# Stick-breaking attention on one core: scores as two products per key block instead of three, and later-key sums taken from softplus tiles that VectorE adds first

## The reference, cut to what matters

```python
def stick_breaking_attention(q, k, v):
    for i in range(S // Q_BLOCK):            # 4 blocks of 128 queries
        L = (i + 1) * Q_BLOCK
        z = jnp.einsum('bhqd,bhkd->bhqk', qb, kb) * inv_sqrt
        mask = s_idx < t_idx
        log1m = jnp.where(mask, -jax.nn.softplus(z), 0.0)
        after = lax.cumsum(log1m, axis=3, reverse=True) - log1m   # sum over the later keys
        logw = jax.nn.log_sigmoid(z) + after
        w = jnp.where(mask, jnp.exp(jnp.where(mask, logw, 0.0)), 0.0)
        outs.append(jnp.einsum('bhqk,bhkd->bhqd', w, vb))
```

## Time and profile before

| | us |
|---|---|
| median of 3 runs | 1657.78 (1657.31 to 1659.21) |
| the profiled execution, its own time | 1656.84 |
| its span, from the first to the last instruction | 1655.0 |
| PE busy (matmul) | 1628.8, 98% of the span |
| DVE busy | 1050.5 |
| ACT busy | 766.2 |
| POOL busy | 732.0 |

### The profile page before, as it was taken

The page is one execution under the profiler, slowest core; times in us unless marked ns, Lnnn a source line. Parts: engine busy times, 40 slices in busy tenths (PEclk is TensorE's granted clock), DMA queues, the critical chain, the costliest instruction groups (busy, mean ns, idle before and its releaser), DMA issues.

```text
span 1655.0 us, 24390 instructions
## 1 busy us (share of the span) xinstructions
PE 1628.8 (98%) x9460; PEld 1399.6 (85%) x9460; DVE 1050.5 (63%) x1396; ACT 766.2 (46%) x1029; POOL 732.0 (44%) x540
## 2 busy tenths in 40 slices
PE   7999999999999999999999999999999999999997
PEld 4787899999988898888888887887888789999887
DVE  6777758999920065578778788775113699996102
ACT  4756455455543355334444546544223445544322
POOL 3342343333376635443543434445444443335663
PEclk9999999999999999999999999999999999999999
DMA  8565223333243333233332323223233323332432
GB/s 290 208 225 179 91 89 115 115 105 115 86 150 105 108 115 121 98 102 102 102 105 87 119 85 115 90 90 97 95 112 119 126 83 117 112 111 82 150 97 68
DMA packets 65127, 193.49 MB, mean 117 GB/s; under 512 B 5984, under 2 KB 8288, under 8 KB 64000
## 3 DMA queue, kind: packets, MB, share of 16 engines
q1 hardware_dynamic: 65024, 192.06, 35.3%
HBM read 183.59 MB, written 8.45 MB: 116 GB/s over the span
## 4 chain that ended last, share of the span: by engine, by line
PE 90%; DVE 7%; ACT 1%; issue 1%; DMA 1%; SPq 0%; DVEq 0%
PE PR L778 18%; PE PR L779 18%; PE PR L784 18%; PE PR L1182 4%; PE PR L1189 4%; PE PR L1184 4%; PE AX L1182 3%; PE AX L1189 3%; PE AX L1184 3%; PE PR L795 1%; PE PR L796 1%; PE PR L794 1%; PE AX L1003 1%; PE AX L1330 1%; PE AX L1334 1%
## 5 line engine op out<-in xcount | busy, mean ns | idle before, releaser
L703 POOL TENSOR_TENSOR wlo<-raw,whi 128x512 fp32r<-128x512 f32 (+1 forms) x456 | 605.8, 1354 | 631.3 <-ACT whi L1461 631.3
L1461 ACT ACTIVATE whi<-raw 128x1024 fp32r<-128x1024 f32 x216 | 225.9, 1052 | 150.0 <-PE PR L784 127.2
L778 PE MATMUL PR<-h3h,whi 128*128 128x512 f32 x608 | 245.5, 404 | 0.0
L779 PE MATMUL PR<-h3l,whi 128*128 128x512 f32 x608 | 240.4, 395 | 0.0
L722 POOL TENSOR_TENSOR wlo<-raw,whi 128x512 fp32r<-128x512 f32 x72 | 119.1, 1675 | 239.8 <-ACT whi L1719 239.8
L784 PE MATMUL PR<-h3h,wlo 128*128 128x512 f32 x608 | 154.2, 395 | 0.0
L1182 PE MATMUL PR<-ch,whi 128*128 128x256 f32 x560 | 136.0, 282 | 2.0 <-DVE gate L2509 1.2
L784 PEld LDWEIGHTS PR<-h3h,wlo 128*128 128x128 f32 x608 | 114.2, 188 | 27.6
L778 PEld LDWEIGHTS PR<-h3h,whi 128*128 128x128 f32 x608 | 114.3, 188 | 26.6 <-issue 1.2
L779 PEld LDWEIGHTS PR<-h3l,whi 128*128 128x128 f32 x608 | 114.4, 188 | 26.4 <-issue 1.0
L1184 PE MATMUL PR<-cl,whi 128*128 128x256 f32 x560 | 135.7, 281 | 0.0
(11 more groups left out here) (480 smaller groups left out, 3619.2 us busy)
## 6 DMA issues: line engine op xcount, KB each, us to landing
raw<-w SPq DMA_DIRECT2D x224, 512.0 KB, 3.4
cond<-wcond SPq DMA_DIRECT2D x48, 512.0 KB, 4.2
raw<-w SPq DMA_DIRECT2D x32, 384.0 KB, 3.2
raw<-w SPq DMA_DIRECT2D x32, 320.0 KB, 2.9
x_keep<-x SPq DMA_DIRECT2D x3, 2048.0 KB, 7.3
x<-x_keep SPq DMA_DIRECT2D x2, 2048.0 KB, 8.4
abc_a<-acum_rows SPq DMA_DIRECT2D x8, 512.0 KB, 3.9
abc_b<-acum_rows SPq DMA_DIRECT2D x8, 512.0 KB, 4.5
```

The lines of the kernel that those rows point to most:

```text
L703: ins = pool.tensor_tensor(wlo[:, j, a:a + n], raw[:, j, a:a + n], whi[:, j, a:a + n], ALU.subtract)
L778: pe.matmul(bank, whi[:, j, w], part_of(oh, k0 + k), start=first and i == 0, stop=False)
L779: pe.matmul(bank, whi[:, j, w], part_of(ol, k0 + k), start=False, stop=False)
L1461: act.activation(whi[:, j, :], raw[:, j, :], ACT.Copy).then_inc(hi_ready, 1)
```

## The change

1. **Rounded keys twice on the partitions.** `kh` becomes `kk` (`kk_even`, `kk_odd`, one [128, 2, 512] tile for each buffer): for head e of the pair, `kk[:, e, :]` holds the rounded keys on the head's own 64 partitions and, copied, on the other 64. `qh` and `ql` become `qq`: `qq[:, e, :]` holds the rounded queries on the head's own 64 partitions and the low queries on the other 64. One matmul over 128 partitions is then high times high plus high times low. The low keys times the rounded queries stay a matmul over 64 partitions. `scores` issues all 128-partition matmuls of a part and then all 64-partition ones.
2. Each tile that was written by one instruction on 128 partitions is written by two on 64 (`in_result`, `qk_low`, `whole_q_low` and the first key and query tiles), and ACT has two more copies for each key tile, with a semaphore `kk_ready` that `scores` waits for.
3. **Later-key sums.** DVE adds softplus tiles after part 0 (`later_sums`): block 2 plus block 3 for the last 128 queries (128 columns at `SUM_1`), and then two 128-column sums with block 1 (256 columns). `az`, `sp`, `sph` and `spl` are longer by 384 columns; ACT rounds these (one more instruction per head), and DVE takes their low part (one more). `later_keys` then uses a sum where it used two or three blocks.

```diff
@@ scores
-                p, r = h // 2, slice(64 * (h % 2), 64 * (h % 2) + 64)
-                pe.wait_ge(qkl_ready, 2 if p == 0 else lows(nth("k", p)))
+                p, e = h // 2, h % 2
+                pe.wait_ge(kk_ready, p + 1)
+                pe.wait_ge(qkl_ready, 4 if p == 0 else 2 * lows(nth("k", p)))
...
                     for j, c in blocks:
-                        for i, (ks, qs) in enumerate(((kh, qh), (kh, ql), (kl, qh))):
-                            mm = pe.matmul(AXf[:, c:c + T - j * P], ks[r, p % 2, j * P:(j + 1) * P], qs[r, p % 2, j * P:T],
-                                           start=j != 3 and i == 0, stop=False, skip_group_check=True)
+                        pe.matmul(AXf[:, c:c + T - j * P], kk[p % 2][:, e, j * P:(j + 1) * P], qq[p % 2][:, e, j * P:T],
+                                  start=j != 3, stop=False, skip_group_check=True)
+                    for j, c in blocks:
+                        mm = pe.matmul(AXf[:, c:c + T - j * P], kl[rows_of(e), p % 2, j * P:(j + 1) * P],
+                                       qq[p % 2][rows_of(e), e, j * P:T], start=False, stop=False, skip_group_check=True)
                     mm.then_inc(z_done, 1)
@@ later_keys
-                for n, (_, _, blocks) in enumerate(PARTS):
-                    for part, ready in ((sph, sph_ready), (spl, spl_ready)):
-                        pe.wait_ge(ready, 2 * h + n + 1)
-                        for j, c in blocks:
-                            mm = pe.matmul(AXf[:, c:c + T - j * P], late[:, 2, :], part[:, c:c + T - j * P],
...
-                            for j2 in range(j + 1, NCH):
-                                c2, off = KCOL[j2], c + (j2 - j) * P
-                                mm = pe.matmul(AXf[:, off:off + T - j2 * P], late[:, 3, :], part[:, c2:c2 + T - j2 * P],
...
+                for part, ready in ((sph, sph_ready), (spl, spl_ready)):
+                    pe.wait_ge(ready, 2 * h + 1)
+                    for j, c in PARTS[0][2]:
+                        add(c, T - j * P, 2, part[:, c:c + T - j * P], stop=part is spl and j == NCH - 1)
+                    add(KCOL[2] + P, P, 3, part[:, KCOL[3]:KCOL[3] + P], stop=part is spl)
+                for part, ready in ((sph, sumh_ready), (spl, suml_ready)):
+                    pe.wait_ge(ready, h + 1)
+                    mm = add(KCOL[1] + P, 2 * P, 3, later_1(part), stop=part is spl)
+                mm.then_inc(cum_done, 1)
+                pe.wait_ge(sph_ready, 2 * h + 2)
+                add(0, T, 2, sph[:, 0:T])
+                add(P, P, 3, sph[:, KCOL[1]:KCOL[1] + P])
+                for part in (sph, spl):
+                    add(2 * P, 2 * P, 3, part[:, SUM_0:SUM_0 + 2 * P])
+                add(P, P, 3, spl[:, KCOL[1]:KCOL[1] + P])
+                pe.wait_ge(spl_ready, 2 * h + 2)
+                mm = add(0, T, 2, spl[:, 0:T], stop=True)
+                mm.then_inc(cum_done, 1)
@@ act, before head 0
-            act.activation(kh[:, 0, :], PR[:, 1, :], ACT.Identity, bias=bias[:, 1:2]).then_inc(qkvu_ready, 1)
+            for e in range(2):
+                ins = act.activation(k_high(0, e), PR[rows_of(e), 1, :], ACT.Identity, bias=bias[rows_of(e), 1:2])
+            ins.then_inc(qkvu_ready, 1)
             h1_high(6)
             h1_high(7)
+            act.wait_ge(qkvu_ready, 1)
+            for e in range(2):
+                ins = act.activation(k_high(0, e, other=True), k_high(0, e), ACT.Copy)
+            ins.then_inc(kk_ready, 1)
@@ act, in_result
+                if kind == 1:
+                    act.wait_ge(qkvu_ready, u + 1)
+                    for e in range(2):
+                        ins = act.activation(k_high(p, e, other=True), k_high(p, e), ACT.Copy)
+                    ins.then_inc(kk_ready, 1)
@@ act, soft
                     act.activation(sph[:, c:c + w], sp_[:, c:c + w], ACT.Copy).then_inc(sph_ready, 1)
+                    if n == 0:
+                        act.wait_ge(later_sum, 2 * h + 2)
+                        act.activation(sph[:, SUM_1:NZL], sp_[:, SUM_1:NZL], ACT.Copy).then_inc(sumh_ready, 1)
@@ dve, soft_plus
+                    if n == 0:
+                        dve.wait_ge(sumh_ready, h + 1)
+                        dve.tensor_tensor(spl[:, SUM_1:NZL], sp_[:, SUM_1:NZL], sph[:, SUM_1:NZL], ALU.subtract).then_inc(
+                            suml_ready, 1)
+            def later_sums(h):
+                dve.wait_ge(sp_ready, 2 * h + 1)
+                dve.tensor_tensor(sp_[:, SUM_1:SUM_1 + P], sp_[:, KCOL[2] + P:NZ], sp_[:, KCOL[3]:KCOL[3] + P],
+                                  ALU.add).then_inc(later_sum, 1)
+                dve.wait_ge(later_sum, 2 * h + 1)
+                dve.tensor_tensor(sp_[:, SUM_0:NZL].rearrange("p (a b) -> p a b", a=2),
+                                  sp_[:, KCOL[1] + P:KCOL[1] + 3 * P].rearrange("p (a b) -> p a b", a=2), later_1(sp_),
+                                  ALU.add).then_inc(later_sum, 1)
```

More of the change, by code:

```diff
@@ L193, in hybrid_blocks @@
             ff2 = sb("ff2", [P, 2, T], F32, over)
+        with ExitStack() as over:
+            kk_odd = sb("kk_odd", [P, 2, T], F32R, over)
         abc_a = sb("abc_a", [P, 2, T])
@@ L207, in hybrid_blocks @@
         rr = sb("rr", [P, T])
+        with ExitStack() as over:
+            pw_odd = sb("pw_odd", [P, NZ - T], F32, over)
         sq = sb("sq", [P, 2, T])
@@ L240, in phase_a @@
                      pooled=a("pooled", [P, T]), wp=a("wp", [P, 4, P]))
-            t.update(ql=a("ql", [P, 2, T], F32R), kl=a("kl", [P, 2, T], F32R),
-                     pw_odd=a("pw_odd", [P, NZ - T]), pfix=a("pfix", [P, 16]), shifts=a("shifts", [P, KT, 2], F32R), bias=a("bias", [P, 8]))
+            t.update(qq_odd=a("qq_odd", [P, 2, T], F32R), kl=a("kl", [P, 2, T], F32R),
+                     pfix=a("pfix", [P, 16]), shifts=a("shifts", [P, KT, 2], F32R), bias=a("bias", [P, 8]))
             return t.values()
-        (mix1, h1h, xn, h1l, mixh, mixl, cond, macc, att, late, az, sp_, sph, spl, qh, kh, vT, vtok, pw, padA, padB, padC, pooled, wp,
-         ql, kl, pw_odd, pfix, shifts, bias) = region(phase_a)
+        (mix1, h1h, xn, h1l, mixh, mixl, cond, macc, att, late, az, sp_, sph, spl, qq_even, kk_even, vT, vtok, pw, padA, padB, padC, pooled, wp,
+         qq_odd, kl, pfix, shifts, bias) = region(phase_a)
+        kk, qq = (kk_even, kk_odd), (qq_even, qq_odd)
         def phase_joint(a):
@@ new lines, in add @@
+                def add(to, w, weights, moving, stop=False):
+                    return pe.matmul(AXf[:, to:to + w], late[:, weights, :], moving, start=False, stop=stop, skip_group_check=True)
+                for part, ready in ((sph, sph_ready), (spl, spl_ready)):
[3 more added lines that the diff above has]
+                    add(KCOL[2] + P, P, 3, part[:, KCOL[3]:KCOL[3] + P], stop=part is spl)
```

60 lines of the change are left out of this document (42 added, 18 removed).

## The result

The changed kernel takes 1662.2 us (median of 9 runs, 1660.41 to 1662.94), the kernel before 1657.59 (9 runs, 1656.22 to 1659.27). The ratio is 1.0028, with a 95% interval of 1.0019 to 1.0036: **slower by 4.6 us**, where the prediction took 3.3 us for what a measurement tells from no change. The forecast was 1660.4, no change. The time lies in its range, but over its own bound for slower (1661.1), to which it gave 0.28, and the loss of 2.6 us was 2 us short.

The account below looks back on a forecast made before the run. The prediction took PE's own instructions to bound attention (57 to 190 us). Losses of 8.65 us less gains of 6.1 gave +2.6: 1659.4 for the profiled execution, 1660.4 for the median, range 1655.0 to 1663.8.

Parts of the forecast that it names:

- PE's gains: PE in attention: 0.57 us per head in later keys plus 1.5 over eight heads in scores, 6.1 us in all.
- changes inside a head are free: Rival: shape changes inside a head's scores cost PE nothing, 4.7 us less on PE; about 1657; chance 0.10.
- changes cost double: Rival: shape changes in scores cost double, or 128-row matmuls behind 64 read PSUM late; about 1663.5; chance 0.10.
- Half the partitions, half the price: Rival: split ACT and DVE instructions on 64 partitions cost half, so early losses shrink; about 1655.4; chance 0.10.
- First loss, before head 0: Before head 0, split tiles and key copies make the last h1l tile late; PE loses 1.8 us.
- Second loss, head 0: Head 0: PE waits 1.5 us for sph, 0.55 for spl and 0.9 for the weights at head 1's scores.
- Third loss, head 1: Head 1's later keys: DVE delivers spl late, PE loses 1.2 us, then 0.3 for weights.
- Heads 2 to 5: Slack of 2 to 3 us between low part and use, no waits; PE wins back 3.1 us.
- Pooled tiles: The last two pool_map: DVE delivers pooled tiles 2 and 3 late, PE loses 1.0 and 0.9 us.
- Weights of heads 5 and 6: Next scores after the shorter later keys of heads 5 and 6 wait for weights, 0.2 + 0.3 = 0.5 us.
- Nothing waits: Rival: copies and halves hide beside PE's units, so all 6.1 us are won; 1651.7; chance 0.08.
- DVE the bound in every head: Rival: 1.3 us more DVE work per head makes split lows late in every head; 1667; chance 0.12.

Follow-up runs that it names:

- e3: Changed kernel with the low-key product over all 128 partitions, so scores has no change of shape inside (output not the reference's); 1660.72 us, ratio 1.0026.
- e8: Changed kernel with mended work order, and in scores all 128-partition matmuls of a head before all 64-partition ones; 1661.24 us, ratio 1.0024.
- e5: Kernel before plus only a delay: four memsets on DVE ahead of the last two h1l tiles; 1664.17 us, ratio 1.0044.
- e1: Kernel before with the later-key sums alone (part 3 of the change), no key copies or split tiles; 1657.64 us, ratio 1.0001.
- e11: Changed kernel with the one-column matmuls of each mod_sum spread behind pairs of matmuls of the next unit; 1669.19 us, ratio 1.0064.

## Why the prediction was right or wrong

**What bounds the kernel: right.** Waits that replace PE's work set the loss, at the places that were named.

**PE's gains: right.** The later keys of head 2 (100.83 to the unit, 103.03) take 2.20 us, before 2.72: 0.52 won, 0.57 forecast. From the unit behind them to pool_map it is 110.56 - 103.03 = 7.53, before 107.33 - 99.49 = 7.84: 0.31 won in the scores of head 3, 0.24 forecast. The price of a change of shape, forecast as 0.197, is 0.17 (e3), and 0.19 where e8 takes two of them away. The Trainium skill, TensorEngine Tiling (Array Packing), Key Properties, says that a change of the tiling mode drains TensorE. The rows of the changed kernel agree: at each of the four changes (109.11, 109.71, 110.14 and 110.56) the weight load starts only together with its own matmul, while in e3, at the same place without a change, it starts at 109.27 for the matmul at 109.50. So the rivals "changes inside a head are free" and "changes cost double" are both out.

**Half the partitions, half the price: wrong, as forecast.** ACT of the changed kernel before head 0:

```profile
55.94 1.37 ACT L1607 ACTIVATE kk_even<-PR,bias 64x512 fp32r<-64x512 f32 x2
...
58.70 1.27 ACT L1613 ACTIVATE kk_even<-kk_even 64x512 fp32r<-64x512 f32 x2
59.99 0.64 ACT L1616 ACTIVATE late<-att 128x512 fp32r<-128x512 f32 x1
60.53 1.25 ACT L1700 ACTIVATE qq_even<-pw 64x512 fp32r<-64x512 f32 x2
...
67.25 1.18 ACT L1629 ACTIVATE kk_odd<-PR 64x512 fp32r<-64x512 f32 x2
...
69.76 0.81 ACT L1661 ACTIVATE az<-AX 128x768 f32<-128x768 f32 x1
...
74.05 0.83 ACT L1670 ACTIVATE sph<-sp 128x768 fp32r<-128x768 f32 x1
```

Two halves take 1.18 to 1.27 us (1.37 where they read PSUM with a bias), one whole tile 0.62 to 0.68: a half costs what the whole did. **But the term was too small all the same.** The two copies move ACT on by 59.99 - 58.70 = 1.29, 0.645 each, and not by the 0.52 that stood between two whole tiles; they don't overlap as those did. ACT's first key tile starts at 55.94 and Abs of head 0 at 69.76, 13.8 us apart, before 66.61 - 58.05 = 8.6: 5.3 more, where 4.0 was worked out. On DVE two halves move it on by 63.33 - 61.89 = 1.44, 0.72 each and not 0.61:

```profile
61.89 1.40 DVE L2284 TENSOR_TENSOR qq_even<-pw,qq_even 64x512 fp32r<-64x512 f32 x2 [1.11 <-ACT qq_even L1700]
63.33 1.41 DVE L2220 SCALAR_TENSOR_TENSOR h1l<-xn,mod,h1h 128x512 fp32r<-128x512 f32 x2
```

**First loss, before head 0: right in kind, too small.** 1.8 was forecast. The first score of the kernel before on PE's timeline:

```profile
64.44 0.44 PE L1003 MATMUL AX<-qh,kh 64*128 64x384 f32 x1
```

From the first h1l matmul to scores it is 65.16 - 60.92 = 4.24, before 64.44 - 62.48 = 1.96: 2.3 lost.

**Second loss, head 0: right in sum, by another way.** The wait for sph should be 1.5 and is not listed; PE came to it late by itself, since it ran at 1.2 GHz from 66.6 to 70.0 us. ACT ends sph at 74.05 + 0.83 = 74.88, and PE starts at 74.93. From scores to later keys: 74.93 - 65.16 = 9.77, before 72.63 - 64.44 = 8.19, 1.6 lost; forecast 1.5 less 0.24. spl and weights: 0.33 and 0.64, forecast 0.55 and 0.9.

**Third loss, head 1: right.** 0.35 + 0.65 = 1.0 for sph and spl together, forecast 1.2; the 0.3 for weights didn't come.

**Heads 2 to 5: right**, no wait. **Pooled tiles: right**, 1.01 and 0.92 against 1.0 and 0.9. **Weights of heads 5 and 6: right in sum**, one wait of 0.52 ahead of head 7's scores (171.31), forecast 0.5.

**What made it 2 us short.** One part is a term of the sum, the price of a split instruction, above. In the profiled execution attention lost 4.5 us instead of 2.6. Of the 1.9 more, 0.5 fall before head 0 and 0.3 in head 0, where the split tiles and copies stand; this is the term that was too small. The rest comes in pieces, and no experiment parts it: 0.3 in head 1, 0.2 from there to the scores of head 6 (157.81, before 156.58), and 0.6 from there to pool_map(3). Part of the loss was hidden by the 1.6 us that came from the early stretch at 1.2 GHz, which this execution of the kernel before happened to have. Behind 190.56 another 0.7 is lost to the end; no experiment looked for that.

The other part is no term at all: the sum takes it that PE runs at 2.4 GHz whatever it waits for. The prediction read PEclk 1.00 over attention and took it for a property of the stretch. In this one profiled execution it did no harm, since the stretch at 1.2 GHz stood where PE would have waited for sph in any case (e3). Where no tile is late, as in e5, it is paid in full.

What the clock takes over many executions can be bounded. 79 runs of the kernel before, by the mean granted clock that is listed with each run:

```
mean clock     runs   median us
0.997, 0.998   35     1655.8
0.996          13     1656.9
0.994, 0.995   31     1658.2
```

3.4 us at 1.2 GHz are 0.001 of the mean clock (1.7 / 1655), and in the table 0.001 goes with about 1 us; not with 1.7, since the mean also counts stretches that cost nothing (in the profile of the kernel before PEclk is 0.50 over the last 5 us, in which PE does nothing). The nine runs of the changed kernel have a mean of 0.9936 (0.992 to 0.996; the profiled one is the fastest and has 0.996), the 79 of the kernel before 0.9960. By the 79 runs the difference of 0.0024 is worth some 2.4 us, by the nine runs of the changed kernel themselves (1660.4 at 0.996, 1662.6 at 0.992) 1.3. At the same listed clock the two kernels are 3.5 us apart: 1660.4 and 1656.9 at 0.996, 1661.7 (three runs) and 1658.2 at 0.994 and 0.995. So **of the 4.6 us, some 1.1 to 2.4 go with the clock, and 2.2 to 3.5 are the waits less the gains**, which the forecast had at 2.6. The runs don't part them more finely. That a wait can bring the clock down, and that this costs time of its own, is shown by e5, where the wait stands alone and is paid twice in the profiled execution, and all five runs are over 6 us above the kernel before; how often the waits of the changed kernel do it was not counted, as only one execution of it was profiled.

**Slips in the working.** The first `qq` should end at 60.98 + 0.6 + 1.07 + 0.53 = 63.18, not 63.26, and PE, 1.6 late, would take sph at 74.2, not 74.36; neither changes the sum by more than 0.15. DVE was idle for 22% of attention (103.92 busy of 133.00), not for a third.

**Rivals.** "Nothing waits" and "DVE the bound in every head" are out by the list of waits. The sums were to win 0.57 a head and cost DVE time, and e1 shows that the pair comes out at zero.

## What to carry to other kernels

Where one engine sets the pace, an edit that saves its work is worth only what its neighbours deliver in time: 5.4 us of PE's work taken away in e3 gave 1.5 at most. Before copies and halves are given to an "idle" engine, follow its queue to the next tile that the critical engine waits for; its idle time lay in heads 2 to 5, and the new work that cost time stood before and in heads 0 and 1. And give a wait of TensorE a second price, because the clock can fall behind it: nothing where the next tile is late in any case (head 0 of the changed kernel), the length of the wait once more in e5, over twice its length in e11 (6.8 us for a wait of 2.7). Read PEclk in short windows behind each wait, and compare runs by their mean clock before a difference of 0.1% is explained.
